# Differential attention: other places for ScalarE's splits and copies and for VectorE's compressions, and three orders at layer boundaries

## The reference

```python
z = x @ w_in
a_b, a_c, a_v, d_q, d_k, d_v, n_q, n_kv, n_g, m_g = jnp.split(z, SPLIT_POINTS, axis=-1)
...
# differential attention: 4 heads, two maps each, block of 128 queries
sc = jnp.einsum('bqhmd,bkhmd->bhmqk', q_i, k).astype(jnp.float32) * scale
sc = jnp.where(kpos[None, :] <= qpos[:, None], sc, -jnp.inf)
p = jax.nn.softmax(sc, axis=-1)
a = p[:, :, 0] - lam * p[:, :, 1]
o = jnp.einsum('bhqk,bkhd->bqhd', a.astype(v.dtype), v)      # then rms_norm
...
# compression of the keys kc (roped) and the values vc of the sparse attention
blocks = kv[:, idx] + pos_emb[None, None, :, None, :]
jax.nn.gelu(flat @ w1, approximate=False) @ w2
```

## Time and profile before

| | |
|---|---|
| median of 3 runs | 2015.85 us (2013.42 to 2018.76) |
| the profiled execution | 2016.05 us |
| its span | 2013.8 us |
| busy: TensorE, VectorE, ScalarE, GpSimd | 1916.7, 1210.4, 953.5, 531.0 us |
| granted TensorE clock over the span | 0.981 |

### The profile page before, as it was taken

The page is one execution under the profiler, slowest core; times in us unless marked ns, Lnnn a source line. Parts: engine busy times, 40 slices in busy tenths (PEclk is TensorE's granted clock), DMA queues, the critical chain, the costliest instruction groups (busy, mean ns, idle before and its releaser), DMA issues.

```text
span 2013.8 us, 35808 instructions
## 1 busy us (share of the span) xinstructions
PE 1916.7 (95%) x14566; PEld 1694.0 (84%) x14566; DVE 1210.4 (60%) x2445; ACT 953.5 (47%) x1708; POOL 531.0 (26%) x674
## 2 busy tenths in 40 slices
PE   6999999999997988999998999999999899999998
PEld 3855778888885847899987989999998799999998
DVE  4989743233347564655577675575748676558473
ACT  4305532232233466544455564464655556456464
POOL 1320100000001442000011322647372232364735
PEclk9999999999999999999998999999999899999998
DMA  9335442222224254655544444445554444544551
GB/s 344 123 115 205 142 157 94 94 94 95 96 93 157 94 199 160 212 184 185 179 160 140 144 138 166 158 157 183 186 177 146 143 134 145 168 147 165 189 180 53
DMA packets 84546, 307.22 MB, mean 153 GB/s; under 512 B 9376, under 2 KB 10656, under 8 KB 84128
## 3 DMA queue, kind: packets, MB, share of 16 engines
q1 hardware_dynamic: 84384, 304.94, 44.7%
HBM read 303.86 MB, written 1.05 MB: 151 GB/s over the span
## 4 chain that ended last, share of the span: by engine, by line
PE 80%; DVE 11%; ACT 6%; issue 2%; DMA 1%; SPq 0%; POOL 0%; ACTq 0%; DVEq 0%
PE pb L534 17%; PE pb L536 17%; PE pb L535 17%; PE pb L507 6%; PE pb L508 6%; PE pb L513 6%; DVE wlo L1880 2%; ACT whi L1229 2%; DMA raw<-wstream 1%; PE pb L585 1%; DVE Y L2126 1%; PE pb L759 1%; PE pb L918 1%; ACT tmpb L1530 1%; ACT tmpb L1635 1%
## 5 line engine op out<-in xcount | busy, mean ns | idle before, releaser
L534 PE MATMUL pb<-Hh,whi 128*128 128x256 f32 (+1 forms) x2304 | 704.1, 306 | 3.4 <-ACT tmpb L1244 2.9
L535 PE MATMUL pb<-Hl,whi 128*128 128x256 f32 (+1 forms) x2304 | 696.8, 302 | 0.0
L536 PE MATMUL pb<-Hh,wlo 128*128 128x256 f32 (+1 forms) x2304 | 696.7, 302 | 0.0
L1880 DVE TENSOR_TENSOR wlo<-raw,whi 128x1024 fp32r<-128x1024 f32 x326 | 424.5, 1307 | 377.5 <-ACT whi L1229 376.9
L1229 ACT ACTIVATE whi<-raw 128x1024 fp32r<-128x1024 f32 x468 | 489.4, 1054 | 316.1 <-PE pb L536 170.3
L2824 POOL TENSOR_TENSOR wlo<-raw,whi 128x256 fp32r<-128x256 f32 x568 | 428.0, 788 | 737.1 <-ACT whi L1229 736.0
L534 PEld LDWEIGHTS pb<-Hh,whi 128*128 128x128 f32 x2304 | 444.4, 193 | 25.0 <-ACT tmpb L1244 3.3
L535 PEld LDWEIGHTS pb<-Hl,whi 128*128 128x128 f32 x2304 | 444.4, 193 | 15.1
L536 PEld LDWEIGHTS pb<-Hh,wlo 128*128 128x128 f32 x2304 | 444.2, 193 | 15.2
L507 PE MATMUL pb<-Hh,whi 128*128 128x256 f32 (+1 forms) x528 | 161.4, 326 | 3.9 <-ACT Hh L1303 2.4
L508 PE MATMUL pb<-Hh,wlo 128*128 128x256 f32 (+1 forms) x528 | 159.0, 322 | 0.0
(11 more groups left out here) (327 smaller groups left out, 2961.6 us busy)
## 6 DMA issues: line engine op xcount, KB each, us to landing
raw<-wstream SPq DMA_DIRECT2D x572, 512.0 KB, 3.7
X<-xin SPq DMA_DIRECT2D x2, 1024.0 KB, 8.7
out<-X SPq DMA_DIRECT2D x8, 128.0 KB, 1.7
CON<-consts SPq DMA_DIRECT2D x1, 926.0 KB, 8.6
VEC<-vecs SPq DMA_DIRECT2D x1, 662.0 KB, 8.9
CON<-consts SPq DMA_DIRECT2D x1, 147.0 KB, 3.7
VEC<-vecs SPq DMA_DIRECT2D x1, 88.0 KB, 2.0
```

The costliest lines, as they stand in the source:

```text
L534: e.matmul(dst, hi, xh, start=k == 0, stop=False)
L535: e.matmul(dst, hi, xl, start=False, stop=False)
L536: i = e.matmul(dst, lo, xh, start=False, stop=k == kt - 1)
L1880: e.tensor_tensor(wlo[:, i, :], raw[:, p % NRAW, :], f32(whi[:, i, :]), ALU.subtract).then_inc(sig("dve_lo", ("lo", p)), 1)
```

## The change

The change moves work in the instruction orders; it adds and removes none.

1. The compressed inputs kc and vc are copied into a place of their own in Y (`unrolled`) instead of the ring of scratch tiles.
2. On ScalarE, the high splits of an item's product, and the copy and square of a finished head, stand ahead of the item's exponents.
3. On VectorE, the compression of kc moves from the end of item 2 to the end of item 3, and that of vc from the end of item 4 to the place behind item 4's rope, ahead of its low splits.
4. In the first feed-forward the row copy "F" on ScalarE moves from the third tile pair to the first.
5. The transposition of the modulation "G" moves from ahead of the second feed-forward to behind its fifth product, into the bank of `pst`, and VectorE's addition with it.
6. In `centered`, VectorE makes no low split past the last tile before that tile's own work; those splits come behind the sum.

```diff
+        def unrolled(l, key):
+            o = 2048 + T * (key[0] == "vc")
+            return Y[:, o:o + T] if key[0] in ("kc", "vc") else slots.at(("r", l, key))[:, 0:T]
...
-                        if l == 0 and pi == 0 and u is ups[FIRST]:
+                        if pi == 0 and u is ups[FIRST]:
                             mod_tr("pst")
...
             widen("r2", T, ("mt", "n3", 7))
-            mod_tr()
             ffn(1, FFN1, T, "n3", "y3")
...
-                        if l == 0 and j == 2:
+                        if l == 0 and j == 0:
                             row(1.25, "F")
...
                 def copied(key, *until):
                     hi_to(("z", l, key))
-                    t = buf(st - (key[0] in ("dk", "dq")), "r", ("r", l, key), *until)
+                    if key[0] not in ("kc", "vc"):
+                        buf(st - (key[0] in ("dk", "dq")), "r", ("r", l, key), *until)
                     w.wait_ge(*on("lin", "z", l, key))
-                    e.activation(t[:, 0:T], slots.at(("lin", "z", l, key))[:, 0:T], ACT.Copy).then_inc(
+                    e.activation(unrolled(l, key), slots.at(("lin", "z", l, key))[:, 0:T], ACT.Copy).then_inc(
...
                 for n in range(11):
+                    if n < len(EARLY) and EARLY[n][0] not in ("values", "hidden"):
+                        hi_to(("z", l, EARLY[n]))
+                    if 0 <= n - 2 < 8 and n % 2:
+                        (result copy and square of head (n - 2) // 2: lines 1637 to 1643, moved up)
                     if n < 8:
                         (exponents: lines 1629 to 1636)
-                    if 0 <= n - 2 < 8 and n % 2:
-                        (the same copy and square)
...
-                        if l == 0 and j == 3:
-                            mod_add("F")
+                        if j == 3:
+                            mod_add("G" if l else "F")
...
             modulated("n3", "r2", 1, 2, 3, 1)
-            mod_add("G")
             ffn(1, FFN1, T, "y3")
...
                     early_rope(n - 1)
+                    if n == 4:
+                        w.wait_ge(*on("r", l, ("vc",)))
+                        compress(1, unrolled(l, ("vc",)))
                     if n < len(EARLY):
                         early(n)
...
-                    if n in (2, 4):
-                        what = EARLY[n // 2 - 1]
-                        w.wait_ge(*on("zr" if n == 2 else "r", l, what))
-                        compress(n // 2 - 1, slots.at(("r", l, what)))
+                    if n == 3:
+                        w.wait_ge(*on("zr", l, ("kc",)))
+                        compress(0, unrolled(l, ("kc",)))
...
-                    lo_to(keys[7])
+                    lo_to(keys[7], 0)
                     tile(7)
```

More of the change, by code:

```diff
@@ L1589, in early @@
                     what = EARLY[i]
[L1590 to L1593, removed]
+                    if what[0] in ("kc", "vc"):
+                        copied(what)
                     elif what[0] == "kdup":
@@ L1628, in scalar @@
                 for n in range(11):
+                    if n < len(EARLY) and EARLY[n][0] not in ("values", "hidden"):
+                        hi_to(("z", l, EARLY[n]))
+                    if 0 <= n - 2 < 8 and n % 2:
+                        h = (n - 2) // 2
+                        w.wait_ge(*on("do", l, h))
+                        e.activation(DQ[:, h, :], slots.at(("do", l, h))[:, 0:T], ACT.Copy).then_inc(sig("act_o", ("doe", l, h)), 1)
+                        t = buf(st, "dsq", ("dsq", l, h), ("dsum", l, h))
+                        w.wait_ge(*on("doe", l, h))
+                        e.activation(t[:, 0:T], DQ[:, h, :], ACT.Square).then_inc(sig("act_sq", ("dsq", l, h)), 1)
                     if n < 8:
@@ L2403, in rope2 @@
                     w.wait_ge(*on("r", l, key))
-                    rope(("z", l, key), dst, slots.at(("r", l, key))[:, 0:T], "cos2", "sin2", TURN2, ("zr", l, key))
+                    rope(("z", l, key), dst, unrolled(l, key), "cos2", "sin2", TURN2, ("zr", l, key))
                 def dd_rope(key):
@@ L2439, in early_rope @@
                         elif what[0] in ("kc", "kdup"):
-                            rope2(what, KD[:, what[1], 0, :] if what[0] == "kdup" else slots.at(("r", l, what))[:, 0:T])
+                            rope2(what, KD[:, what[1], 0, :] if what[0] == "kdup" else unrolled(l, what))
                 def early(i):
```

## The result

| | before | changed |
|---|---|---|
| median | 2016.43 us (4 runs, 2013.42 to 2018.76) | 1998.26 us (4 runs, 1992.15 to 2000.88) |
| ratio, 95% interval | | 0.9906 (0.9892 to 0.9920) |
| profiled execution | 2016.05 us, span 2013.8 | 1992.15 us, span 1990.2 |

The change makes the kernel faster by 18 us of medians. The profiled execution gains 23.9, because it is the fastest of the changed kernel's four. Readers should keep both: the profile tells where the time went, and the medians how much of it a typical run sees.

A forecast was written before the change was run, and what follows sets the result against it. TensorE, busy for 95% of the span, bounds the kernel, so only its idle and half-clock time can be won. Terms -6.5 - 10.0 - 4.8 + 0.3 - 3.3 + 0.2 = -24.1 us take 2016.05 to 1992, range 1984 to 2004.

The forecast's parts named there:

- step (e): Layer 0, item 5: the 1.34 us wait before head 1's sums is the same order as in (b) and goes.
- (a): Layer 0, item 2: high split ahead of the exponents releases head 0's value product earlier, 1.1 of 1.83 us.
- (b): Layer 0: head 0's copy and square ahead of item 3's exponents, so its sums no longer wait, 2.7 us.
- (c): Layer 0: the values product runs at full clock once the sums' stall is gone, 1.3 us taken of 1.6.
- (d): Layer 0: moved compression of item 1 runs during the values product, so the hidden product's 2.4 us wait goes.
- least slack: Layer 0: both compressions still pass through VectorE, then the engine with least slack; a cost of 1.0 us.
- Step (f): Layer 0, item 6: half clock regained, 1.4 us taken of 2.2.
- the credit: Second feed-forward: modulation's matmuls leave a mostly covered place (1.38 us) and cost 0.6 us in the stream; net +0.3.
- A: Attention: VectorE and GpSimd slow each other, stages give 3 to 6 us instead of 16.5; 2002 to 2005; chance 0.09.
- B: Only the boundaries pay, removed attention waits are replaced on VectorE's chain; 7.6 us left, 2008.5; chance 0.04.
- C: Item 6: ScalarE's splits wait for late weight transfers; slower from 12 us held a layer, 2022 at 15; chance 0.04.
- D: Attention: transfers become the limit and take back its gain; 2008 at most; chance 0.03.

The follow-up runs named there:

- run 9: Changed kernel with the next weight's high split behind the exponents again, the old order of the splits: 2004.97 us, ratio 0.9934.
- run 8: Changed kernel with a finished head's copy and square behind the exponents and also the next product's work, later than before the change: 2006.20 us, ratio 0.9953.
- Run 7: Changed kernel with the two compressions back at the ends of items 2 and 4, own buffer kept: 1995.32 us, ratio 0.9902.
- Run 3: Changed kernel with ScalarE's copy of the hidden row ahead of item 5's exponents instead of behind them: 1992.14 us, ratio 0.9899.
- run 5: Changed kernel with the hidden row's copy ahead of item 5's exponents and item 4's probabilities ahead of the low splits: 1989.49 us, ratio 0.9866.
- run 6: Kernel of run 5 with ScalarE's three high splits at item 4 behind the value copies and the copy for head 1's value product: 1990.67 us, ratio 0.9880.
- run 1: Kernel before with only the attention half of the change (parts 1 to 3), boundaries as before: 2004.54 us, ratio 0.9948.
- run 12: Kernel of run 5 with the boundary orders of run 10 taken back too: 1992.19 us, ratio 0.9890.
- run 10: Changed kernel with the modulation back ahead of the second feed-forward and the old low split order in all norms but layer 0's first: 1995.00 us, ratio 0.9888.

## Why the prediction was right, and which of its steps were not

It said 1992.0, in 1984 to 2004. The median is 1998.3; the profiled execution took 1992.15. The sum was made against one profiled execution, and came out near one. That it came out so near is in part luck: the two stages gave 3.5 us less than forecast, and layer 1's first norm (2.8 us) and the start of the execution (1.1 us), for which the sum had next to nothing, made up for it. Terms against the profile, in us:

| term | predicted | profile | |
|---|---|---|---|
| layer 0's stage | -6.5 | -4.1 | step (e), VectorE's lateness |
| layer 1's stage | -10.0 | -8.9 | the same, hidden by the clock |
| row copy | -4.8 | -4.8 | right |
| modulation | +0.3 | +0.8 | mis-sized |
| layer 0's first norm | -3.3 | -3.1 | right |
| layer 0's second norm, layer 1's first | +0.2 | +0.85 and -2.8 | small term; clock |

**Layer 0, step by step.** (a) held: 1.1 predicted, 0.95 of wait gone, with run 9 to show that the split does it (1.83 us there). (b) held: the 2.70 us went, and run 8, with the square later still, brought such waits back. (c) held: no half-clock patch lies on the values product any more. (d) held as far as it goes: the wait of 2.40 us for the compression went. What failed is what was to be late next. The prediction gave VectorE's least slack 1.0 us; item 4's probabilities were late by 2.21, because the compression, the low splits at 1.71 us each and the gates all stood ahead of them. Run 7 shows that this wait is the old one in another place.

**Step (e) failed.** The prediction took the 1.34 us of head 1's sums for the order of (b). It read only that ScalarE ended it, and not which copy: line 1611 in the earlier trace rows is the hidden row's copy, not the square's line 1643. The copy and square came early and the wait stayed, at 1.63 us. Run 3 removed it by moving that one copy. The row named the cause before the change, and was read past.

**Step (f) failed as well.** Behind the two waits the clock stayed low from 1074 to 1084 for a loss of 3.4 us, as much as before at item 6. With the waits gone in run 5 half of this loss is gone. The prediction had set against (f) a patch of 1.4 us that would stay, so its clock terms stand for 1.3 us in all, and 1.7 came. The waits are what it got wrong: the terms (a), (b), (d), (e) less the two new waits make 5.2 us, and 2.0 were measured. The new wait of head 1's value product was forecast with its cause: 1.3 us, measured 1.81; run 6 removed it.

**Layer 1.** The 2.1 us of item 7's probabilities went, and run 9 shows that it was the split behind the table loads. But the 8.9 us are near the 10.0 by another road than the prediction's. It had 7.3 us of waits and 2.7 of clock; the trace has 3.8 of waits and 5.1 of clock (0.86 to 0.94).

**The boundaries.** In all twelve profiles with the modulation row copied early the first feed-forward is 4.8 us shorter (4.78 to 4.85), and in run 1, without it, 0.04. The wait and the half clock behind it were both counted rightly. At layer 0's first norm eight of the profiles gain 2.87 us up to the sum and four 1.4 to 1.6; with the small matmuls behind it they gain 2.2 to 4.2, around the 3.3 predicted, and run 1 with the old order nothing. At its second norm the variance is held 0.1 us longer, as forecast; the rest of the 0.85 falls on the small matmuls behind it, which ran at half clock. The modulation's price in the stream was right: from its start at 827.50 to the next product at 828.31 it adds 0.58 us. What failed is the credit. Nothing came back where it had stood, since the first product starts 2.47 us behind the small matmuls of line 684 (680 before) in both traces:

```profile
808.14 1.10 PE L684 MATMUL pb<-tmpb,CON 128*128 128x64 f32 x8 [1.02 <-DVE tmpb L1914]
810.61 0.55 PE L511 MATMUL pb<-Hh,whi 128*128 128x256 f32 x1 [1.36 <-ACT Hh L1306]
```

**The signs.** Both stages were to be near 52 us and came to 54.6 and 53.6. The wait of the sums was to go in both layers, and that of head 1 stayed. None of the three signs of being wrong came: no stage above 56 us, no clock under 0.9, and no wait of ScalarE for weights in either stage.

**The rivals.** A has a true mechanism and a small size. GpSimd's quarter splits ran from 1069.15 on, and beside them VectorE's two splits took 3.42 us (1.22 each elsewhere) and a multiplication of one column 0.49 instead of 0.16.

```profile
1069.15 5.18 POOL L2829 TENSOR_TENSOR wlo<-raw,whi 128x256 fp32r<-128x256 f32 x4 [0.87 <-ACT whi L1232]
```

VectorE's busy time in the stages rose by 1.1 and 0.6 us, not by 3.5. The Trainium skill, "SBUF — State Buffer" (section "SBUF: two separate sides"), says that such an operation of VectorE and one of GpSimd take the shared port pair in turn, each for a whole instruction; the trace agrees in kind, since both engines' operations got longer there (GpSimd's four took 5.18 us; most of its others in the stages took 0.7 to 0.9 each). B fell: the attention gave 10.8 us of medians in run 1. C and D did not come: the DMA queue's waits for the hidden product to free raw buffers are 21.4 us in all, 23.5 before, and the stages ran with the data engines at 48%.

**Why medians gain less than the profile.** Each run has its granted clock on record. The changed kernel's four took 1992.15 us at 0.985, 1997.67 at 0.984, 1998.85 at 0.983 and 2000.88 at 0.979; run 12's five went from 1984.84 at 0.989 to 1998.07 at 0.981. Same instructions, other half-clock patches; a thousandth of clock is 2 us, so the clock tells most of the spread and not all of it (1992.15 and 1997.67 differ by one thousandth). Layer 1's first norm shows it in the profiles: against before it came out at -2.7, about -1.4 (three times), 0.2 (three times) and 1.6 to 1.8 (six times), with the old order of the split in the second and the last group. The 2.8 us of the changed kernel's profile lie at the end of that spread.

## What to carry to other kernels

Read the line that ends a wait, not only its engine: two waits that look alike may hang on different copies, and the second may be a bank that another user still holds. When a wait is removed, follow what is queued behind the moved work until each engine's next deadline; here two waits in series hid each other, and each fix alone gave nothing that the time showed. Compare a part's wait with what undoing the part costs: the compressions' wait was 2.4 us and undoing their move cost under 1 us a layer. Then check that the undoing is exact, and take the clock's loss out of both sides before the waits are compared: in layer 0 it was 5.1 of 8.7 us of "costs".

## What the runs showed of the hardware

Losses by the clock come in steps. In short slices of the span outside its two ends, each kernel's lost time (length times one less the granted clock) sits in separate patches of 1.70 us or a multiple of it: before has fourteen such places, run 12 ten. A slice wholly inside one shows a granted clock of 0.50, which is 1.2 GHz (1078 to 1082 us of the changed kernel), slices at the edges a mixture of 1.2 and 2.4. In layer 0's stage of before both stand behind waits of the earlier trace rows. The same instructions met 0.981 in one run and 0.989 in another. The Trainium skill, "TensorE: Matmul & The Clock Gate" (Part 1), says that the gate runs on its own and is not reset when a kernel starts, so that one kernel measures different numbers of slow matmuls from run to run; the runs here agree, with a spread of 13 us in run 12. With two to six runs the intervals above are 0.0025 to 0.0044 wide, 5 to 9 us. A change that is worth under 4 us, like the boundary orders of run 10, therefore needs the waits of the trace to be told; five runs do not tell it.
